# Expert look-ups and one-hots of a PEER layer in other forms, and its last thirty-two row dots at another place in the stream

## What is computed

```python
q = (tb @ w_q).reshape(PEER_BLOCK, PEER_HEADS, 2, PEER_HALF)
s = jnp.einsum('thik,hink->thin', q, sub_keys)            # 2 x 128 scores per head
s_top, i_top = lax.top_k(s, PEER_TOPK)                    # 16 best of each half
cand = s_top[:, :, 0, :, None] + s_top[:, :, 1, None, :]
best_s, best_c = lax.top_k(cand.reshape(...), PEER_TOPK)  # 16 best pairs
i1 = jnp.take_along_axis(i_top[:, :, 0], best_c // PEER_TOPK, axis=-1)
i2 = jnp.take_along_axis(i_top[:, :, 1], best_c % PEER_TOPK, axis=-1)
eid = i1 * N_KEYS + i2
g = jax.nn.softmax(best_s, axis=-1)
act = jax.nn.gelu(jnp.einsum('thkd,td->thk', u_tab[eid], tb))
out = jnp.einsum('thk,thkd->td', g * act, v_tab[eid])
```

## Time and profile before

| | |
|---|---|
| median of 3 runs | 2279.7 us (2272.84 to 2282.3) |
| the profiled execution's own time | 2277.83 us |
| its span in the trace | 2276.1 us |
| PE busy | 2229.8 us, 98% of the span |
| POOL busy | 1475.2 us, 65% |
| DVE busy | 1585.5 us, 70% |
| ACT busy | 814.1 us, 36% |

### The profile page before, as it was taken

One profiled execution on the slowest core, in us unless ns is written; L12 is line 12 of the kernel. 1 busy time (PEld: TensorE's weight loads), 2 busy tenths in 40 slices (PEclk: granted clock), 3 DMA queues, 4 the chain that ended last, 5 costly groups with the idle time before them and its releaser, 6 DMA issues.

```text
span 2276.1 us, 38281 instructions
## 1 busy us (share of the span) xinstructions
PE 2229.8 (98%) x14510; PEld 2152.9 (95%) x14510; DVE 1585.5 (70%) x2800; ACT 814.1 (36%) x1201; POOL 1475.2 (65%) x851
## 2 busy tenths in 40 slices
PE   8999999999999999999999999999989999999998
PEld 8999999997799999999999999999989999999998
DVE  7866444546678336768978889898478777777774
ACT  4443223432133002133433344444344444444442
POOL 5554333432354555557878887889778888888873
PEclk9999999999999999999999999999999999999999
DMA  6224323225763233248888897999999999999982
GB/s 215 84 80 137 97 92 101 93 96 194 250 230 128 84 126 94 84 132 275 304 286 289 291 313 248 300 331 318 355 364 396 374 369 374 385 370 375 381 311 79
DMA packets 212800, 535.19 MB, mean 235 GB/s; under 512 B 16816, under 2 KB 101168, under 8 KB 210224
## 3 DMA queue, kind: packets, MB, share of 16 engines
q1 hardware_dynamic: 111392, 234.65, 31.7%
q0 software_dynamic: 46080, 167.79, 19.7%
q10 hardware_dynamic: 55184, 130.77, 15.7%
HBM read 453.89 MB, written 79.25 MB: 234 GB/s over the span
## 4 chain that ended last, share of the span: by engine, by line
PE 85%; DVE 7%; POOL 2%; DMA 2%; ACT 1%; issue 1%; ACTq 0%; DVEq 0%; SPq 0%; POOLq 0%
PE ps L1008 47%; PE ps L732 30%; PE ps L1066 2%; POOL w_lo L706 1%; DVE prev L1875 1%; PE ps L909 1%; DMA gbuf<-gate_scratch 1%; POOL ug L698 1%; PE ps L896 1%; PE ps L904 1%; PE ps L1021 1%; PE ps L913 1%; PE ps L929 1%; DVE n_lo L1991 1%; DVE oh L2097 1%
## 5 line engine op out<-in xcount | busy, mean ns | idle before, releaser
L673 POOL TENSOR_SCALAR w_hi<-raw 128x1024 fp32r<-128x1024 f32 x129 | 139.5, 1081 | 516.3 <-issue 384.0
L706 POOL TENSOR_TENSOR w_lo<-raw,e_hi 128x1024 fp32r<-128x1024 f32 x128 | 326.4, 2550 | 95.2 <-PE ps L1008 85.3
L706 POOL TENSOR_TENSOR w_lo<-raw,w_hi 128x1024 fp32r<-128x1024 f32 x128 | 318.9, 2492 | 86.6 <-PE ps L1008 84.5
L1008 PE MATMUL ps<-p_hi,w_lo 128*128 128x416 f32 x1024 | 361.4, 353 | 0.0
L1008 PE MATMUL ps<-g_hi,w_lo 128*128 128x416 f32 x1024 | 359.6, 351 | 0.0
L675 POOL TENSOR_TENSOR w_lo<-raw,w_hi 128x1024 fp32r<-128x1024 f32 x129 | 320.7, 2486 | 10.8
L732 PE MATMUL ps<-h_hi,w_hi 128*128 128x288 f32 (+2 forms) x1216 | 273.0, 306 | 1.6 <-ACT ma L1342 1.6
L732 PE MATMUL ps<-h_lo,w_hi 128*128 128x288 f32 (+2 forms) x1216 | 262.1, 297 | 0.0
L732 PE MATMUL ps<-h_hi,w_lo 128*128 128x288 f32 (+2 forms) x1216 | 261.7, 296 | 0.0
L2075 DVE CUSTOM_DVE_ANT_0 ug<-ug,ps 128x1024 f32<-128x1024 f32 x160 | 192.3, 1213 | 72.2 <-DMA ug<-rows_u,eid 56.4
L698 POOL DMA_INDIRECT ug<-rows_u,eid x160 | 214.8, 1342 | 37.5 <-issue 24.3
(11 more groups left out here) (358 smaller groups left out, 5086.0 us busy)
## 6 DMA issues: line engine op xcount, KB each, us to landing
raw<-units SPq DMA_DIRECT2D x385, 512.0 KB
gate_scratch<-gt SPq DMA_DIRECT2D x52, 512.0 KB
activation_scratch<-ge ACTq DMA_DIRECT2D x120, 208.0 KB
abuf<-activation_scratch ACTq DMA_DIRECT2D x30, 832.0 KB
gbuf<-gate_scratch ACTq DMA_DIRECT2D x30, 832.0 KB
prev<-ssm_in ACTq DMA_DIRECT2D x8, 1024.0 KB, 6.7
ssm_s<-prev ACTq DMA_DIRECT2D x8, 1024.0 KB, 4.5
cxb<-parked_tiles ACTq DMA_DIRECT2D x8, 870.0 KB, 6.8
```

The source lines that it names most:

```text
L673: pool.tensor_scalar(w_hi[:, s, :], raw[:, r, :], 1.0, 1.0, ALU.mult, ALU.mult).then_inc(s_whi, 1)
L706: pool.tensor_tensor(w_lo[:, n % 2, :], raw[:, n % RAW, :], e_hi[m % HS_].bitcast(F32), ALU.subtract)\
L1008: last = mm(accp[par], w[:, k * P:(k + 1) * P], x_[:, k, t0:t0 + ND], start=k == 0 and i == 0, stop=k == KT - 1 and i == 2)
```

## The change

1. One-hots. Two DVE instructions of 4096 elements in a block become four of 2048: the plain one-hot of the second key, the one-hot of the first key (now in an array `oh_a` of its own), the product with the first part of the weight, and the product with the second part in place of the plain one-hot. Row dots lie between them. `keyb` and `partb` lose their order by blocks.
2. Spread dots. Of the 32, 20 (`N_BESIDE`) move beside the last ten gate blocks, two in each. The first 128 dots therefore end with block 13 (2 or 3 in a block in place of 1 or 2), blocks 14 and 15 have none. PE turns the spread tokens once more, into banks 2 and 3, after the products of block 15, when the 128 dots have been done; DVE waits for that before block 16's dots. The other 12 stay behind the blocks: 6 at once, 6 singly. The dues of these rows in `rows_in_order` change as well.
3. ACT's copy of the next scores moves from `n // 2 + 2` to `2 * n // 3 + 1` units into a stretch of n, the exponential from `3 * n // 4 + 1` to `7 * n // 8 + 1`: from 16 to 18 units in the stretches of 20, from 8 to 9 in the last one, of 10.
4. Look-ups. The arrays are float16 in place of bfloat16, with pairs of picks innermost. The comparison becomes two instructions of 2048 elements, a copy of the keys in pairs (512 elements) is added, the product stays 4096, and the sum over 16 becomes additions of 2048, 1024, 512 and 256.

```diff
-DOTS_B = [(b + 1) * (N_PICK - N_SEARCH) // NB - b * (N_PICK - N_SEARCH) // NB for b in range(NB)]
-DOTS_U = [9, 0, 0, 1, 1, 1, 1, 1, 1]
-DOTS_V = [2, 2, 2, 2, 2, 2, 3, 2]
+N_BESIDE = 20
+B_SPREAD = NB - N_BESIDE // 2
+DOTS_B = shares(N_PICK - N_SEARCH, B_SPREAD - 2) + [0, 0] + shares(N_BESIDE, NB - B_SPREAD)
+N_TAIL = N_PICK + N_BESIDE
+DOTS_U = [6, 0, 0, 1, 1, 1, 1, 1, 1]
+DOTS_V = [0] * GI
...
-    use += [(k, TAIL + (k - N_PICK) * 2 * GI // (N_ROW - N_PICK)) for k in range(N_PICK, N_ROW)]
+    use += [(k, TAIL + (0 if u < 0 else GI // 2 + u // 2 if u < GI else u)) for u in range(-1, 2 * GI) for k in tail_dots(u)]
...
                 gates(b, b % 2, b == 0)
+                if b == B_SPREAD - 1:
+                    pe.wait_ge(s_ud, N_PICK)
+                    turn_rows(1, spread_columns, h_beside)
...
-                    if m == m0 + (n // 2 + 2 if j else n - 1) and j + 1 < len(TT):
+                    if m == m0 + (2 * n // 3 + 1 if j else n - 1) and j + 1 < len(TT):
                         scores_out(j + 1)
-                    if j and m == m0 + 3 * n // 4 + 1:
+                    if j and m == m0 + 7 * n // 8 + 1:
                         act.wait_ge(s_be, PARTS + j)
...
-                tt_(oh[:, par, 1:3].rearrange("p i a k c -> p (i a) k c"), across, keys_, ALU.is_equal).then_inc(s_eq, 1)
+                tt_(plain, across, key_b, ALU.is_equal).then_inc(s_eq, 1)
+                tt_(oh_a[:, par], across, key_a, ALU.is_equal)
                 for k in due[0:1]:
                     row_dot(k)
                 dve.wait_ge(s_eq, b + 1)
-                tt_(oh[:, par, 0:2], plain, weights, ALU.mult).then_inc(s_oh, 1)
-                for k in due[1:]:
+                tt_(oh_w[:, par, 0], plain, weight[0], ALU.mult)
+                for k in due[1:2]:
+                    row_dot(k)
+                tt_(plain, plain, weight[1], ALU.mult).then_inc(s_oh, 1)
+                for k in due[2:]:
                     row_dot(k)
...
-                link(tt_(met, bself[:, :, 0:np_].unsqueeze(3).to_broadcast(shape),
-                         marks[:].unsqueeze(2).to_broadcast(shape), ALU.is_ge))
+                for i in range(2):
+                    last = tt_(met[:, i], bself[:, i, 0:np_].rearrange("p (a c) -> p a c", c=2).unsqueeze(2)
+                               .to_broadcast(shape), marks[:, i].unsqueeze(1).to_broadcast(shape), ALU.is_ge)
...
-                link(dve.tensor_reduce(pick[:, 0:2, picked], met, AX.X, ALU.add))
+                for n in (TOPK // 2, TOPK // 4, TOPK // 8):
+                    link(tt_(folded[:, :, 0:n], folded[:, :, 0:n], folded[:, :, n:2 * n], ALU.add))
+                link(tt_(pick[:, 0:2, picked].rearrange("p i (a c) -> p i a c", c=2),
+                         met[:, :, :, 0], met[:, :, :, 1], ALU.add))
```

90 lines of the change are left out of this document (50 added, 40 removed).

## The result

The changed kernel takes 2299.1 us (median of 6 runs, 2295.4 to 2302.7) against 2278.3 us of the kernel before (6 runs, 2272.8 to 2282.3): ratio 1.0089, 95% interval 1.0076 to 1.0101, 20.8 us slower. The forecast was 2274 us, 0.25% faster, with a range of 2262 to 2293. It was wrong in its direction and in its size.

What follows compares the result with a forecast made beforehand. PE, busy 98% of the span, was taken as the bound. Terms -7 + 2.5 + 6 + 0.9 + 2 - 10.5 = -6.1 us turned the median of 2279.7 into 2274 us, range 2262 to 2293.

Steps and rivals of the forecast that it cites:

- Look-ups: In the full searches, shorter DVE instructions hold POOL up less, so PE loses less: gain 7 us of 10.0.
- third rival: Look-ups go on holding POOL up through more instructions with two SBUF operands; the 7 us stay lost, 2281 us, chance 0.12.
- Exponential: One unit later in the last search, DVE goes on 4.5 us later with 2.0 covered: cost 2.5 us.
- Turn: One more turn of the spread tokens on PE in the gate blocks: cost 0.9 us, its waits over when reached.
- Start of `v`: After 1640 us, fewer gathers and dots let gates land sooner; PE's wait and low clock go: gain 10.5 us.
- fourth rival: The start of `v` isn't relieved because SP's `raw` loads fill the freed queues: 2284 us, chance 0.08.
- Unit 123: Six gathers behind this unit make the next `w_lo` 4 us late, partly covered by a PE wait: cost 2 us.
- Gate blocks: POOL's and DVE's losses together 8 us, less 1.9 already lost: cost 6 us, ends -2 and 25.
- POOL: In the gate blocks, units with three gathers delay `w_lo`: about 6 us lost, gathers taking 1.7 us.
- DVE: First 14 gate blocks take 10.4 us against PE's 9.4; a lead of one block covers 9, leaving 5 us.
- Rows: In the gate blocks, rows land in 4.6 us within 6.6 to 7.9 of room, so the shorter lead costs nothing.
- first rival: Rows land late in the gate blocks as added gathers load the queues: 19 us lost, 2293 us, chance 0.15.

Runs made afterwards that it cites:

- ten dots beside: Changed kernel with ten spread dots beside the gate blocks for twenty, dues evenly spaced, exponential and scores as before: 2275.9 us, ratio 0.9988.
- with rows on time: Changed kernel with gathers issued two units earlier only for rows due in the gate blocks: 2295.1 us, ratio 1.0070.
- the run of round 1: Changed kernel with the spread dots, their dues and the turns as in the kernel before, the rest changed: 2272.5 us, ratio 0.9973.
- with and without lead: Gathers for gate-block rows two units earlier or not: whole dots 2295.1 against 2299.1 us, dots over 256 columns 2274.0 against 2284.3 us.
- short dots: Changed kernel with gate-block dots over 256 of the 1024 columns, gathers unchanged: 2284.3 us, ratio 1.0020; with gathers two units earlier too, 2274.0 us.

## Why the prediction was wrong

**Look-ups: right.** -6.6 us for -7, 6.9 by the medians of two kernels that differ in nothing else, and 103, 103 and 101 products in 20 us for the "over 102" that was to show it. But of the single durations only the comparison's was as forecast. The changed kernel's first full look-up:

```profile
1099.54 2.57 DVE L2172 COPY keyd<-keyd 128x512 f16<-128x512 f16 x1
1102.04 2.35 DVE L2177 TENSOR_TENSOR eq<-bself,marks 128x2048 f16<-128x2048 f16 x2
1104.42 4.40 DVE L2181 TENSOR_TENSOR eq<-eq,keyd 128x4096 f16<-128x4096 f16 x1
```

The copy took 2.57 us for 0.5, beside a `w_lo` that had begun 0.1 us ahead of it, and the product 4.40 for 2.28, while `w_lo` beside it took 2.71 in place of 4.99: now DVE is held up and POOL isn't. That is where PE's time came from. The third rival, that POOL stays held up, is refuted.

**Exponential: right where it was read**, 2.2 us in one pair of runs and 2.8 in the other, for 2.5. DVE stood 6.90 us for ACT there, 6.13 before. The other 1.6 of the +3.8 are there with the early exponential too: block 0's 32 products took 3.21 and 3.34 us in these two runs and 2.01 in the kernel before, behind the same wait of 1.99 us. In the whole time neither pair shows it: 2272.5 and 2271.7 us with the dots as before, and the changed kernel was no faster.

**Turn** is in the 25.1 us. **Start of `v`: nearly right**, -8.4 us for -10.5, and the fourth rival is refuted; 241 products stand in 50 us from 1672 on for 199, and the DMA share is 0.86 for 0.99. Its sign came true: the load of the second group's gates that had taken 16.73 us, the first half's, landed in 7.0:

```profile
L1556 ACTq DMA_DIRECT2D gbuf<-gate_scratch x1: 577/577/577, 1692.8 to 1692.8; - x1
...
DMA to landing us min/median/max: 7.0/7.0/7.0
```

The 15.09 us in the changed kernel's chain are the second half's, and PE waited 0.8 us behind them. With ten dots beside, where one dot a unit stays in this stretch, the same unit wins 7.9 us, nearly as much. **Unit 123**: +4.5 us for +2, outside its ends of 0 and 4, and not by a late `w_lo`.

**Gate blocks: the step that failed**, +25.1 us with the turn for 6.9, at the far end of the range I had given. What failed is the overlap: DVE's time was to be covered by a lead of one block, and rows were to land within it. The working had three parts.

- *POOL*, 6 us: nothing came of it. PE waited 1.8 us for `w_lo` in the whole stretch, as much as before. The gathers took what was forecast, 1.57 us for 1.7:

```profile
L711 POOL DMA_INDIRECT ug<-rows_u,eid x51 | 80.1, 1571 | 12.4 <-issue 7.5 <-DVE dots L2088 2.4 <-PE ps L1021 1.5
```

- *DVE*, 5 us. The block came out as forecast, 10.50 us measured with rows on time for 10.4, but in part by luck: POOL held the one-hots up for 2.8 us and not 2.2 (2.0, had I taken the mean of the group in the earlier trace rows, 3.14 us, and not its median of 3.34), while each instruction begins 0.08 us before the one ahead of it is done, which the sum left out. What failed is "DVE can be one block ahead, which covers 9". It can, but it wasn't: it ended block 1's one-hots at 1381.7 us, and PE began that block's products at 1382.9: it started with a lead of 1.2 us, 2.7 if PE had taken a mean block. And "from block 16 on 9.5 just fits" measured 10.4 in that run for blocks 17 to 24, since the one-hots took 8.43 us and not 7.1. A cover has to be read at the point where it is first used.

- *Rows*, "I take the former", landing in 4.6 us. It was this that I had to choose, and the choice was wrong. My 4.6 and the 6.6 to 7.9 of room count from the end of the gather's instruction on POOL. The profile's own landing times count from its start: in the changed kernel's gate blocks 8.1 us in the median, of which the instruction is 1.57 in the mean, so about 6.5 by my count (an estimate from these two); the four on its chain of waits 9.56, 7.81, 8.97 and 7.34, or 7.8, 6.9, 7.2 and 5.6 by my count:

```profile
ug<-rows_u,eid POOLq DMA_INDIRECT x51, 8.1
```

```profile
1410.09 9.56 DMA ug<-rows_u,eid
1449.30 7.81 DMA ug<-rows_u,eid
1483.86 8.97 DMA ug<-rows_u,eid
1518.96 7.34 DMA ug<-rows_u,eid
```

The trace of the kernel before had it: of 21 rows that DVE waited for in the searches 4.6 is nearly the least, and the most is 6.7, here 7.70 us from the start of the gather or 6.74 from its end:

```profile
1147.53 0.96 POOL L698 DMA_INDIRECT ug<-rows_u,eid  x1 [0.15 <-issue]
```

```profile
1155.23 1.22 DVE L2075 CUSTOM_DVE_ANT_0 ug<-ug,ps 128x1024 f32<-128x1024 f32 x1 [1.81 <-DMA ug<-rows_u,eid]
```

With the dots where they stood before, landing in the gate blocks is nearly the same, only hidden by seven units of lead (the run of round 1, 35 gathers):

```profile
ug<-rows_u,eid POOLq DMA_INDIRECT x35, 7.9
```

The room was wrong as well. It was counted up to where PE wants the gates; but DVE works in order and had no time to spare, so a row is late as soon as DVE wants it. It wanted the four it waited for 3.7, 0.3, 4.8 and 4.8 us after the end of their gathers. Three of these gathers stand behind a `w_lo` that had itself waited 9.2 to 11.5 us for PE: a late block makes the next rows late.

So the first rival was right in what happened: rows come late, and the time ends beyond its 2293 us. It was wrong in two things. Landing doesn't grow with the number of the gathers in the stretch (7.9 and 8.1 us at 35 and 51), so the added gathers had no part in it; whether the DMA share had, 0.93 and 0.90 in these two stretches, can't be told, since it is high in both. And late rows are only a part of the 25 us, 4 to 10 by the medians of the pairs with and without lead; it gave them 19 and had no room for the rest.

**What no step had** is that the dots lie between the one-hots. The order was in front of me (two dots ahead of the last one-hot), and I looked at it only for who waits for what. The prediction priced meetings with POOL as a constant, 2.2 us a block. They are 2.8 with the dots between and 1.9 with the dots together, and since DVE bounds the stretch by then, each of them is paid. With rows on time the order alone is 18.1 - 0.7 = 17.4 us in the gate blocks and 19.9 by the medians; with late rows 25.1 - 5.1 = 20.0, and 18.1 by the medians. That is more than 14 x 0.9 = 13 us. In blocks 17 to 24 the block on DVE fell from 10.41 to 9.99 us, which is another 3; for the rest I have no run.

In the kernel with two instructions of 4096 elements (spread dots alone) the same 24 us are lost in another way: PE waits 14.6 us for `w_lo` in 11 places. The order was not tried there, and nothing shows how much of its loss is late rows.

## What to carry to other kernels

When an engine nears its bound, its instructions' durations are no constants: look at which of them are held up by a neighbour and how they alternate with those that aren't, and put like with like before moving work. A cover is worth what it is at the first moment it's needed; read how far the engine is ahead there, not how far its buffers would let it be. And when a hidden transfer loses its lead, take its landing time from the stretch where it will be exposed, from many of its transfers and not from one, and count it from the same point as the room that it has to fit; if the trace shows it nowhere, carry the bad end of the range in the forecast, not in a rival.

## What the runs showed that I had not expected

Two crossed pairs of runs (lead, short dots) added up within 0.1 us in the profiled executions, which the medians don't bear out, and named a cause that a change of order, with as much work, took away for the most part. Even a true sum would have shown only that the two changes work on different things, not that nothing else works on both.

Issuing gathers earlier is no free gain: in the searches two units more lead made POOL wait 51.4 us for dots and cost 22.4 us, since `w_lo` stands behind the gather in the same queue.
